# The down weights' three quarters move from GpSimd's DMA queue to SyncE's

## The chip, the cores and the metric

The kernel runs on one core of one Trainium2 chip. The metric is the device time of one execution in microseconds (us). A core has TensorE (PE, with its weight loads as PEld), VectorE (DVE), ScalarE (ACT), GpSimd (POOL) and SyncE (SP). SP computes nothing in this kernel; it issues DMAs. Its DMAs stand in the profile as queue q1 (hardware_dynamic), those that GpSimd issues as queue q0 (software_dynamic).

## The reference, cut to what matters

Two transformer blocks follow one another on 256 tokens of width 1024, all in fp32. What matters here is the feed-forward part of each, with D_FF = 2816 in the first block and 4096 in the second:

```python
# first block
g = h @ w_gate; u = h @ w_up
x = x + (silu(g) * u) @ w_down
# second block
hid = square(relu(n2 @ w_up)); mlp_out = hid @ w_down
h = h + rms_norm_2(mlp_out, norm_mlp_post)
```

Ahead of each feed-forward part stand norms, projections and attention, which the change does not touch.

## The kernel before, in words

Every fp32 operand is split into a rounded part ("hi") and the rest ("lo"), and each product is three matmuls: hi by hi, hi by lo, lo by hi. ACT rounds a weight block, DVE subtracts ("cuts") the lo part, PE multiplies.

Most weights come in "fills" of 512 KB. `sync_program` issues them in one written order on SP's queue, into four raw buffers `w_raw`; fill k waits until fill k-4 has been cut (L524), which frees its buffer. Each is rounded in `round_fill` (L1431) and cut in `cut_fill` (L2163).

The down weights come in another way. A "pair" is 256 rows of w_down by its 1024 columns. `quarters` lays a pair out as four quarters of 128x512. The product of a pair with the hidden rows is formed as a two by two product with seven instead of eight block products, which needs sums of quarters. So a pair is loaded by three DMAs, all on GpSimd's queue:

- `load_twice(q)` (L3349) writes the fourth quarter twice into `pair_t` (512 KB; shown as pair_sums).
- `load_pair(q)` (L3359) writes the three others into `pair_raw[i]` (768 KB). There are two such buffers, i = 0 (shown as pair_raw) and i = 1 (a part of `tmp`), used in turn. It waits until all three parts of pair q-2 have been cut, since pair q-2 lay in the same buffer.
- `add_pair(q)` (L3365) waits for the first to land, and adds quarters 0 and 1 onto it in the DMA (512 KB read, with accumulate).

ACT rounds a pair in three parts (`round_pair`, L1770): part 0 the three quarters, part 1 the two sums of the DMAs, part 2 two more sums that DVE has made (L2644, L2650). DVE cuts each part (`cut_pair`, L2628). The last pair of the first block and the last two of the second are "quartered": multiplied plainly, without sums. Pairs 0 to 10 belong to the first block (PAIRS1 = 11, LAST1 = 10), pairs 11 to 26 to the second (FIRST2 = 11, LAST2 = 26).

Every engine runs a written, in-order program. In the two feed-forward loops PE does for each pair its up products (L972: four fills a pair in the first block, `up1`, two in the second, `up2`), and the down products of an earlier pair (L1018); quartered pairs are multiplied on L1037. ACT takes the finished up products out of PSUM in `take_up` (L1808) or `take_hidden` (L2081), between its roundings, and PE waits for that (`up_taken`) before it writes the same bank again. In the second block's loop DVE's order for pair q, in iteration i = q - FIRST2 + 1, is

```python
cut_pair(q, 0); sum_pair(q); cut_hidden(q); sum_pair_rest(q)
cut_pair(q, 1)
cut_fill(k)        # k = first fill of up2 + 2 i + 4
cut_pair(q, 2)
cut_fill(k + 1)
```

and in the first block's loop, iteration i = q + 1, with f the first fill of up1, it ends in `cut_fill(f+4i+5)`, `cut_hidden`, `cut_pair(q, 1)`, `cut_pair(q, 2)`, `scale_gate`, `cut_fill(f+4i+6)`.

Of the kernel before, what the change touches and what calls it, by code (L numbers as in the profile page):

```python
# [40 lines left out]
PAIRS1, PAIRS2 = D_FF // (2 * P), D_FF2 // (2 * P)  # L41
# [95 lines left out]
class Weights:  # L137
# [82 lines left out]
    def used(self, name):  # L220
# [18 lines left out]
inverted_a ratio_b dens_b summed_b  # L239
x_added  # L240
spread_done spread_copied gate_scaled acted hidden_done hidden_rounded hidden_cut hidden_summed up_taken
pair_landed0 pair_landed1 twice_landed0 twice_landed1 pair_added0 pair_added1 pair_summed pair_rounded pair_cut pair_used product_done quarter_done first_copied mixed_read formed
v_gelued v_centred v_mean v_root v_scaled v_done u_done spatial_done gated_u
rows2_copied rows2_done v2_act v2_dve scored2 masked gmax_done smax_done
exped2 turned2 copied2_act copied2_dve attended2 yb_done gate_summed sigmoided
# [1 line left out]
vector_step pool_step  # L247
""".split()
Semaphores = namedtuple("Semaphores", SEMAPHORES + ["w_landed", "x_landed", "turned_landed", "post_landed", "stored", "pair_landed",
                                                   "twice_landed", "pair_added"])  # L250


def program(nc, a, out):
    with ExitStack() as ctx:
        T = Names()
        sems = {name: ctx.enter_context(nc.semaphore(name)) for name in SEMAPHORES}
        S = Semaphores(w_landed=[sems[f"w_landed{r}"] for r in range(RAW_SLOTS)],
                       x_landed=[sems[f"x_landed{t}"] for t in range(TILES)],
                       turned_landed=[sems[f"turned_landed{n}"] for n in range(KC // 2)],
                       post_landed=[sems[f"post_landed{t}"] for t in range(TILES)],  # L260
                       stored=[sems[f"stored{t}"] for t in range(TILES)],
                       pair_landed=[sems[f"pair_landed{n}"] for n in range(2)],
                       twice_landed=[sems[f"twice_landed{n}"] for n in range(2)],
                       pair_added=[sems[f"pair_added{n}"] for n in range(2)], **sems)
        allocate(nc, ctx, T)
        W = Weights(a)
        sync_program(nc, a, out, T, S, W)
        tensor_program(nc, T, S, W)
        scalar_program(nc, a, out, T, S, W)
        vector_program(nc, T, S, W)  # L270
        pool_program(nc, a, T, S, W)
# [167 lines left out]
LAST1, FIRST2, LAST2 = PAIRS1 - 1, PAIRS1, PAIRS1 + PAIRS2 - 1  # L439
# [3 lines left out]
def pair_parts(q):  # L443

    return 3 * q - sum(p < q for p in QUARTERED)


def pairs_summed(q):

    return q - sum(p < q for p in QUARTERED)  # L450


def pairs_used(q):

    return q - sum(p < q for p in QUARTERED)


def quarter_place(q, y):


    buf = pair_place(q)[0]
    return (1 - buf, y + 4) if q == LAST2 and y < 3 else (buf, y)


def pair_loads(q):

    return 16 * sum(pair_place(p)[1] == pair_place(q)[1] for p in range(q + 1))


def pair_adds(q):  # L470

    return 16 * sum(pair_place(p)[1] == pair_place(q)[1] for p in range(q + 1) if p not in QUARTERED)


def pair_place(q):

    i = q if q <= LAST1 else q - FIRST2
    return (i + 1) % 2, i % 2
# [12 lines left out]
def rows_of(out):  # L491

    return out[0].rearrange("(m s r) d -> s m r d", s=TILES, r=2)
# [12 lines left out]
def sync_program(nc, a, out, T, S, W):  # L506
    sp = nc.sync
    rows_out = rows_of(out)

    sp.dma_start(T.w_raw[:, 0:1, 0:WIDE], W.half).then_inc(S.half_landed, 16)  # L510
    for k, pieces in enumerate(W.fills):
        r = k % RAW_SLOTS
        if 0 < k < KC // 2:
            sp.dma_start(T.xt[:, 2 * k:2 * k + 2, :], a["turned"][:, 2 * k:2 * k + 2, :]).then_inc(S.turned_landed[k], 16)
        if k == RAW_SLOTS:
            sp.dma_start(T.vectors[:], a["vectors"]).then_inc(S.vectors_landed, 16)
        if k == RAW_SLOTS + 2:
            sp.dma_start(T.small[:], a["small"]).then_inc(S.small_landed, 16)
            sp.dma_start(T.xm[:], a["meta_tokens"]).then_inc(S.meta_landed, 16)
            sp.dma_start(T.rope1m[:], a["rope1m"]).then_inc(S.small_meta_landed, 16)  # L520
            for t in range(TILES):
                sp.dma_start(T.x[:, t, :], a["x"][0, t * P:(t + 1) * P, :]).then_inc(S.x_landed[t], 16)
        if k >= RAW_SLOTS:
            sp.wait_ge(*W.cut(S, k - RAW_SLOTS))  # L524
        for view, src in pieces:
            sp.dma_start(view(T.w_raw[:, r, :]), src).then_inc(S.w_landed[r], 16)
    for t in range(TILES):
        for half in range(2 - t):
            cols = slice(half * WIDE, (half + 1) * WIDE)
            sp.wait_ge(S.x_posted, 4 + 2 * t + half + 1)  # L530
            sp.dma_start(rows_out[t][:, :, cols], T.x[:, t, cols]).then_inc(S.stored[t], 16)
    for t in range(TILES):
        sp.wait_ge(S.stored[t], 32)
# [881 lines left out]
def scalar_program(nc, a, out, T, S, W):  # L1415
    act, bank = nc.scalar, T.bank
# [334 lines left out]
    def round_pair(q, part):  # L1751

        buf, i = pair_place(q)
        if part == 0:
            act.wait_ge(S.pair_landed[i], pair_loads(q))
            if q == 1:
                act.wait_ge(S.w_used, W.first["up1", 2])
            elif q == FIRST2:
                act.wait_ge(S.quarter_done, 4)
            elif q == FIRST2 + 1:  # L1760
                act.wait_ge(S.w_used, W.first["up2", 4])
            elif q > 1:
                act.wait_ge(S.pair_used, pairs_used(q - 1))
        elif part == 1:
            act.wait_ge(S.pair_added[i], pair_adds(q))
        else:
            act.wait_ge(S.pair_summed, pairs_summed(q) + 1)
        places, src = ((slice(0, 3), T.pair_raw[i]), (slice(3, 5), T.pair_t[:, i]),
                       (slice(5, 7), T.pair_raw[i][:, 0:3:2, :]))[part]
        act.activation(T.pair_hi[buf][:, places, :], src, ACT.Copy).then_inc(S.pair_rounded, 1)  # L1770

    def round_quarters(q, part):

        i = pair_place(q)[1]
        if part == 0:
            act.wait_ge(S.pair_landed[i], pair_loads(q))
            act.wait_ge(S.pair_used, pairs_used(LAST2 - 2 if q == LAST2 else q - 1))
        else:
            act.wait_ge(S.twice_landed[i], pair_loads(q))
            if q == LAST2:  # L1780
                act.wait_ge(S.product_done, 2 * len(MIXED))
        buf, y = quarter_place(q, 3 * part)
        n, src = ((3, T.pair_raw[i]), (1, T.pair_t[:, i, 0:1, :]))[part]
        act.activation(T.pair_hi[buf][:, y:y + n, :], src, ACT.Copy).then_inc(S.pair_rounded, 1)
# [35 lines left out]
    f = W.first["up1", 0]  # L1820
# [277 lines left out]
    f = W.first["up2", 0]  # L2098
# [14 lines left out]
    for i in range(2, PAIRS2 - 1):  # L2113
        q = FIRST2 + i - 1
        k = f + 2 * i + 4
# [1065 lines left out]
def pool_program(nc, a, T, S, W):  # L3181
    pool = nc.gpsimd
# [156 lines left out]
    def load_twice(q):  # L3339

        i, n = pair_place(q)[1], 1 if q in QUARTERED else 2
        if q == 0:
            pool.wait_ge(S.cut_done, CUT["h2"] + 4)
        elif q == FIRST2:
            pool.wait_ge(S.attended2, TILES * HEADS2)
            pool.wait_ge(S.x_added, 12)
        elif q not in (1, FIRST2 + 1):
            pool.wait_ge(S.pair_cut, pair_parts(q - 2) + 2)
        pool.dma_start(T.pair_t[:, i, 0:n, :], W.pairs[q][:, 3:4, :].broadcast_to([P, n, WIDE])).then_inc(S.twice_landed[i], 16)  # L3349

    def load_pair(q):
        i = pair_place(q)[1]
        if q == 1:
            pool.wait_ge(S.x_squared, 4)
        elif q == FIRST2 + 1:
            pool.wait_ge(S.x_squared, 8)
        elif q not in (0, FIRST2):
            pool.wait_ge(S.pair_cut, pair_parts(q - 1))
        pool.dma_start(T.pair_raw[i], W.pairs[q][:, 0:3, :]).then_inc(S.pair_landed[i], 16)  # L3359

    def add_pair(q):

# [2 lines left out]
        pool.dma_start(T.pair_t[:, i], W.pairs[q][:, 0:2, :], accum_op=ALU.add).then_inc(S.pair_added[i], 16)  # L3365

    load_twice(0)
    load_pair(0)
    load_twice(1)
    add_pair(0)  # L3370
    add_pair(1)
    load_pair(1)
    load_const(0)
    for q in range(2, PAIRS1):
        load_twice(q)
        load_pair(q)
        if q < LAST1:
            add_pair(q)
        if q - 1 < CONST_DMAS:
            load_const(q - 1)  # L3380
# [17 lines left out]
    pool.dma_start(T.bg[1][:], a["norm_mlp_post_2"][0:1, :].broadcast_to([P, D])).then_inc(S.post_landed[1], 16)  # L3398
    pool.wait_ge(S.w_used, W.first["o", 1])
    load_twice(FIRST2)  # L3400
    load_pair(FIRST2)
    load_twice(FIRST2 + 1)
    for t in range(TILES):
        pool.wait_ge(S.post_mean, t + 1)
# [2 lines left out]
    add_pair(FIRST2 + 1)  # L3407
    pool.wait_ge(S.x_mean, 4)
    root(T.row_scale[:, 3, :]).then_inc(S.x_root, 1)
    load_pair(FIRST2 + 1)  # L3410
    for q in range(FIRST2 + 2, LAST2 + 1):
        load_twice(q)
        load_pair(q)
        if q not in QUARTERED:
            add_pair(q)
    for t in range(TILES):
# [20 lines left out]
```

## Time and profile before

| | |
|---|---|
| median of 3 runs | 741.71 us (741.19 to 744.46) |
| the profiled execution | 742.65 us, its span 741.3 us |
| busy PE, DVE, ACT, POOL | 97%, 76%, 58%, 20% of the span |
| DMA | 149.34 MB, mean 201 GB/s |
| queue q1 (SP) | 96.68 MB, 38.6% of the 16 DMA engines' span |
| queue q0 (GpSimd) | 51.39 MB, 25.4% |
| first feed-forward loop | about 141 to 313 us |
| second feed-forward loop | about 562 to 735 us |

A row of the timeline gives the start and the duration of an instruction, and in brackets how long its engine had been idle before it and what ended that. A DMA instruction's duration is the time to issue it; the time "to landing" is from its issue until its data are there.

### The profile page before, as it was taken

To read this page: it belongs to the slowest core of one execution; us is meant where nothing else is said; L and a number is where in the kernel's file an instruction comes from. 1 tells how busy PE (TensorE), PEld (TensorE's weight loads), DVE (VectorE), ACT (ScalarE), POOL (GpSimd) and SP (SyncE) were. 2 spreads that over 40 slices of the span, in tenths; PEclk is the share of its full clock that TensorE was granted. 3 is DMA by queue.
4 is the path that set the end of the run, shared out by engine and by line. 5 is a ranking of instruction groups with operands and counts; after the bars stand their busy time and mean duration, and the time that the engine had idled before them with its cause. 6 is when DMAs were issued, how large, how long until landed. Compare 5 with 4: busy or idle time off the path is not lost.

```text
span 741.3 us, 11216 instructions
## 1 busy us (share of the span) xinstructions
PE 720.9 (97%) x4322; PEld 625.3 (84%) x4322; DVE 561.9 (76%) x817; ACT 432.9 (58%) x610; POOL 150.0 (20%) x200
## 2 busy tenths in 40 slices
PE   6999999999999999999999999999999999999996
PEld 5877778999999999888888888888778989999995
DVE  5899695689888778966747654675758899988875
ACT  6756763567665566476443444564356777767652
POOL 3867551312211110001110000000312122211200
PEclk9999999999999999999999999999999999999999
DMA  9642233699988886256536643374569799999721
GB/s 311 217 138 86 61 134 114 224 296 331 313 265 260 262 258 219 79 174 223 172 112 197 187 152 118 113 241 129 174 222 277 205 300 300 296 294 267 199 80 57
DMA packets 51750, 149.34 MB, mean 201 GB/s; under 512 B 4993, under 2 KB 6225, under 8 KB 51697
## 3 DMA queue, kind: packets, MB, share of 16 engines
q1 hardware_dynamic: 38672, 96.68, 38.6%
q0 software_dynamic: 12592, 51.39, 25.4%
q8 instruction: 34, 0.56, 0.3%
q10 hardware_dynamic: 432, 0.56, 0.2%
q14 instruction: 20, 0.16, 0.1%
HBM read 147.49 MB, written 1.05 MB: 200 GB/s over the span
## 4 chain that ended last, share of the span: by engine, by line
PE 84%; DVE 8%; DMA 5%; ACT 1%; issue 1%; POOL 0%; SPq 0%; DVEq 0%; ACTq 0%
PE psum L972 24%; PE psum L549 23%; PE psum L1018 14%; PE psum L602 11%; PE psum L1037 2%; DMA pair_sums<-in_down 2%; DVE w_lo L2163 2%; DMA w_raw<-in_w_in 2%; PE psum L776 1%; PE psum L697 1%; PE psum L642 1%; PE psum L727 1%; PE psum L1181 1%; DMA w_raw<-in_w_out 1%; DVE w_lo L2628 1%
## 5 line engine op out<-in xcount | busy, mean ns | idle before, releaser
L2163 DVE TENSOR_TENSOR w_lo<-w_raw,w_hi 128x1024 fp32r<-128x1024 f32 x171 | 209.9, 1237 | 31.6 <-ACT w_hi L1431 31.1
L1431 ACT ACTIVATE w_hi<-w_raw 128x1024 fp32r<-128x1024 f32 x177 | 184.6, 1055 | 47.0 <-DMA w_raw<-in_w_in 38.5
L972 PE MATMUL psum<-h_hi,w_hi 128*128 128x256 f32 x608 | 169.7, 283 | 2.3 <-ACT up_rows L2081 1.6
L972 PE MATMUL psum<-h_hi,w_lo 128*128 128x256 f32 x608 | 169.0, 282 | 0.0
L972 PE MATMUL psum<-h_lo,w_hi 128*128 128x256 f32 x608 | 163.3, 282 | 0.0
L972 PEld LDWEIGHTS psum<-h_hi,w_hi 128*128 128x128 f32 x608 | 114.4, 188 | 4.6 <-ACT up_rows L2081 2.1
L972 PEld LDWEIGHTS psum<-h_hi,w_lo 128*128 128x128 f32 x608 | 114.5, 188 | 0.0
L972 PEld LDWEIGHTS psum<-h_lo,w_hi 128*128 128x128 f32 x608 | 111.2, 188 | 1.3 <-DVE h_lo L2183 0.2
L549 PE MATMUL psum<-w_hi,h_hi 128*128 128x512 f32 (+1 forms) x240 | 94.5, 394 | 0.0
L549 PE MATMUL psum<-w_hi,h_lo 128*128 128x512 f32 (+1 forms) x240 | 92.9, 387 | 0.0
L549 PE MATMUL psum<-w_lo,h_hi 128*128 128x512 f32 (+1 forms) x240 | 92.9, 387 | 0.0
L549 PEld LDWEIGHTS psum<-w_hi,h_lo 128*128 128x128 f32 x240 | 45.1, 188 | 10.0
L602 PE MATMUL psum<-w_hi,h_hi 128*128 128x512 f32 x128 | 52.7, 412 | 0.4 <-DVE tmp L2896 0.4
L549 PEld LDWEIGHTS psum<-w_lo,h_hi 128*128 128x128 f32 x240 | 45.2, 188 | 9.3
L549 PEld LDWEIGHTS psum<-w_hi,h_hi 128*128 128x128 f32 x240 | 45.2, 188 | 9.2
L602 PE MATMUL psum<-w_lo,h_hi 128*128 128x512 f32 x128 | 50.5, 394 | 0.0
L3349 POOL DMA_DIRECT2D pair_sums<-in_down x27 | 19.2, 712 | 137.2 <-DVE pair_lo L2628 59.2
L602 PE MATMUL psum<-w_hi,h_lo 128*128 128x512 f32 x128 | 46.7, 395 | 0.0
L1808 ACT ACTIVATE up_rows<-psum 128x512 f32<-128x512 f32 x22 | 13.1, 594 | 53.1 <-PE psum L972 53.1
L1770 ACT ACTIVATE w_hi<-tmp 128x1536 fp32r<-128x1536 f32 (+1 forms) x24 | 30.5, 1270 | 19.0 <-DVE tmp L2650 9.9
L3365 POOL DMA_DIRECT2D pair_sums<-in_down x24 | 21.2, 882 | 94.6 <-DMA pair_sums<-in_down 94.6
L1770 ACT ACTIVATE pair_hi<-pair_raw 128x1536 fp32r<-128x1536 f32 (+1 forms) x24 | 30.5, 1273 | 16.4 <-DVE pair_raw L2650 9.7
(346 smaller groups left out, 1392.7 us busy)
## 6 DMA issues: line engine op xcount, KB each, us to landing
w_raw<-in_w_in SPq DMA_DIRECT2D x77, 512.0 KB, 4.6
w_raw<-in_up SPq DMA_DIRECT2D x76, 512.0 KB, 6.2
pair_sums<-in_down POOLq DMA_DIRECT2D x48, 512.0 KB, 6.9
pair_raw<-in_down POOLq DMA_DIRECT2D x14, 768.0 KB, 7.9
tmp<-in_down POOLq DMA_DIRECT2D x13, 768.0 KB, 8.1
w_raw<-in_w_out SPq DMA_DIRECT2D x16, 512.0 KB, 3.7
w_raw<-in_w_branch_a SPq DMA_DIRECT2D x4, 512.0 KB, 4.1
w_raw<-in_w_branch_b SPq DMA_DIRECT2D x4, 512.0 KB, 4.8
```

Source lines behind the costliest of these rows:

```text
L549: mm = pe.matmul(bank[b][:, 0:width], x[:, kc, t * P:(t + 1) * P], y[:, h * width:(h + 1) * width], start=first and n == 0, stop=last and ...
L602: mm = pe.matmul(out, x[:, kc, t * P:(t + 1) * P], y, start=n == 0 and i == 0, stop=last and i == 2)
L642: mm = pe.matmul(bank[7][0:32 + META, :], T.meta_stack[:, kc, :], y, start=kc == 0 and n == 0, stop=kc == KC - 1 and n == 1)
L972: mm = pe.matmul(out, x, y[:, kc, :], start=kc == 0 and n == 0, stop=kc == KC - 1 and n == last_pass)
L1018: mm = pe.matmul(bank[b][:], u, v, start=first and n == 0, stop=last and n == 2)
L1037: mm = pe.matmul(bank[b][:], u, v, start=first and b == 7 and c == 0 and n == 0, stop=last and c == 1 and n == 2)
L1431: act.activation(T.w_hi[:, W.slot[k], :], T.w_raw[:, k % RAW_SLOTS, :], ACT.Copy).then_inc(S.w_rounded, 1)
L1770: act.activation(T.pair_hi[buf][:, places, :], src, ACT.Copy).then_inc(S.pair_rounded, 1)
L1808: act.activation(T.rows[:, j % 2, :].rearrange("p (c n) -> p c n", c=2), src, ACT.Copy).then_inc(S.up_taken, 1)
L2163: dve.tensor_tensor(T.w_lo[:, W.slot[k], :], T.w_raw[:, k % RAW_SLOTS, :], T.w_hi[:, W.slot[k], :], ALU.subtract).then_inc(S.w_cut, 1)
L3349: pool.dma_start(T.pair_t[:, i, 0:n, :], W.pairs[q][:, 3:4, :].broadcast_to([P, n, WIDE])).then_inc(S.twice_landed[i], 16)
L3365: pool.dma_start(T.pair_t[:, i], W.pairs[q][:, 0:2, :], accum_op=ALU.add).then_inc(S.pair_added[i], 16)
```

## The change

`load_pair` is split in two. The first two pairs of each block (0, 1, 11, 12) stay on GpSimd's queue, under the name `load_first`, with the same waits, and count on semaphores of their own (`first_landed`). All other pairs (2 to 10 and 13 to 26) are loaded by SP, between its fills, with the same wait for the cuts of pair q-2. `ahead` says ahead of which fill: f+4q+6 in the first block (f the first fill of up1), and in the second the first fill of up2 + 2(q-11) + 7. Where that fill doesn't exist (pairs 24, 25, 26), the loads follow the last fill. `pair_there` gives ACT the semaphore and count of a pair. `load_twice` and `add_pair` are as before.

```diff
+FIRSTS = (0, 1, FIRST2, FIRST2 + 1)
+def pair_there(S, q):
+    i, same = pair_place(q)[1], FIRSTS if q in FIRSTS else [p for p in range(q + 1) if p not in FIRSTS]
+    return (S.first_landed if q in FIRSTS else S.pair_landed)[i], 16 * sum(p <= q and pair_place(p)[1] == i for p in same)
 ...
 def sync_program
+    def load_pair(q):
+        i = pair_place(q)[1]
+        sp.wait_ge(S.pair_cut, pair_parts(q - 1))
+        sp.dma_start(T.pair_raw[i], W.pairs[q][:, 0:3, :]).then_inc(S.pair_landed[i], 16)
+    ahead = {W.first["up1", 0] + 4 * q + 6: q for q in range(2, PAIRS1)}
+    ahead.update({W.first["up2", 0] + 2 * (q - FIRST2) + 7: q for q in range(FIRST2 + 2, LAST2 + 1)})
     for k, pieces in enumerate(W.fills):
+        if k in ahead:
+            load_pair(ahead[k])
 ...
+    for k in sorted(ahead):
+        if k >= len(W.fills):
+            load_pair(ahead[k])
 ...
 round_pair and round_quarters, part 0
-            act.wait_ge(S.pair_landed[i], pair_loads(q))
+            act.wait_ge(*pair_there(S, q))
 ...
 pool_program
-    def load_pair(q):
+    def load_first(q):
         i = pair_place(q)[1]
         if q == 1:
             pool.wait_ge(S.x_squared, 4)
         elif q == FIRST2 + 1:
             pool.wait_ge(S.x_squared, 8)
-        elif q not in (0, FIRST2):
-            pool.wait_ge(S.pair_cut, pair_parts(q - 1))
-        pool.dma_start(T.pair_raw[i], W.pairs[q][:, 0:3, :]).then_inc(S.pair_landed[i], 16)
+        pool.dma_start(T.pair_raw[i], W.pairs[q][:, 0:3, :]).then_inc(S.first_landed[i], 16)
 ...
     for q in range(2, PAIRS1):
         load_twice(q)
-        load_pair(q)
         if q < LAST1:
             add_pair(q)
 ...
     for q in range(FIRST2 + 2, LAST2 + 1):
         load_twice(q)
-        load_pair(q)
         if q not in QUARTERED:
             add_pair(q)
```

## Rows read from the trace of the kernel before

**Rows 1.** Busy time by stretch, first block's loop and second block's loop: start:end, length, busy by engine.
```profile
158.00:299.50 141.50, 141.09 (x1019) 133.21 (x1020) 119.54 (x157) 88.71 (x110) 22.98 (x34) 1.00 0.86 277
563.00:607.50 44.50, 43.01 (x302) 39.83 (x300) 41.57 (x54) 33.58 (x42) 9.66 (x13) 1.00 0.88 260
607.50:723.80 116.30, 116.15 (x760) 106.26 (x761) 103.74 (x122) 79.85 (x89) 21.62 (x31) 1.00 0.80 237
```
**Rows 2.** The chain of waits from 595 us: start, length, what.
```profile
602.02 1.68 DVE w_lo L2628
...
607.02 0.59 ACT up_rows L2081
...
607.65 5.96 PE psum L972 x48
...
713.25 5.69 PE psum L972 x48
```
**Rows 3.** All waits, 563 to 724 us: who for whom, us in total, times, longest.
```profile
POOL tmp L3359 <- DVE w_lo L2628: 10.0, 7, 1.5
ACT w_hi L1770 <- DMA tmp<-in_down: 1.8, 1, 1.8
PE psum L972 <- ACT up_rows L2081: 1.6, 1, 1.6
```
**Rows 4.** DVE timeline, 588 to 591 us: the cuts that free buffers.
```profile
588.02 1.22 DVE L2163 TENSOR_TENSOR w_lo<-w_raw,w_hi 128x1024 fp32r<-128x1024 f32 x1
589.16 1.22 DVE L2628 TENSOR_TENSOR w_lo<-tmp,w_hi 128x1024 fp32r<-128x1024 f32 x1
590.29 1.22 DVE L2163 TENSOR_TENSOR w_lo<-w_raw,w_hi 128x1024 fp32r<-128x1024 f32 x1
```
**Rows 5.** Issues of SP and POOL, and the time to landing of the load at 590.67.
```profile
589.27 0.33 SPq L526 DMA_DIRECT2D w_raw<-in_up  x1
590.67 0.56 POOL L3359 DMA_DIRECT2D tmp<-in_down  x1 [1.54 <-DVE w_lo L2628]
591.54 0.33 SPq L526 DMA_DIRECT2D w_raw<-in_up  x1
609.72 0.56 POOL L3359 DMA_DIRECT2D tmp<-in_down  x1 [1.53 <-DVE w_lo L2628]
...
DMA to landing us min/median/max: 9.7/9.7/9.7
```
**Rows 6.** ACT timeline: pair rounding, and the fill of 591.54 rounded.
```profile
588.92 1.47 ACT L1770 ACTIVATE pair_hi<-pair_raw 128x1536 fp32r<-128x1536 f32 x1
600.36 1.49 ACT L1770 ACTIVATE w_hi<-tmp 128x1536 fp32r<-128x1536 f32 x1 [1.82 <-DMA tmp<-in_down]
608.17 1.05 ACT L1431 ACTIVATE w_hi<-w_raw 128x1024 fp32r<-128x1024 f32 x1
```
**Rows 7.** DMA issues of two windows, KB and us to landing: fills of 589.27, 591.54.
```profile
w_raw<-in_up SPq DMA_DIRECT2D x1, 512.0 KB, 6.4
...
w_raw<-in_up SPq DMA_DIRECT2D x1, 512.0 KB, 9.0
```
**Rows 8.** The second block's first moved pair: its issue by POOL, SP's fill, DVE's cut.
```profile
575.24 0.56 POOL L3359 DMA_DIRECT2D pair_raw<-in_down  x1 [0.45 <-DVE pair_lo L2628]
578.39 0.33 SPq L526 DMA_DIRECT2D w_raw<-in_up  x1
592.41 1.75 DVE L2628 TENSOR_TENSOR pair_lo<-pair_raw,pair_hi 128x1536 fp32r<-128x1536 f32 x1
```
**Rows 9.** Busy time by stretch, second block, last two columns DMA share and GB/s.
```profile
589.00:600.40 11.40, 11.40 (x78) 10.46 (x78) 11.30 (x14) 7.35 (x10) 2.51 (x5) 1.00 0.91 264
```
**Rows 10.** First block: pair 3's load by POOL, its rounding by ACT, last pair's wait.
```profile
174.75 0.55 POOL L3359 DMA_DIRECT2D tmp<-in_down  x1 [0.42 <-DVE w_lo L2628]
188.92 1.48 ACT L1770 ACTIVATE w_hi<-tmp 128x1536 fp32r<-128x1536 f32 x1
716.49 1.49 ACT L1784 ACTIVATE pair_hi<-tmp 128x1536 fp32r<-128x1536 f32 x1 [0.61 <-DMA tmp<-in_down]
```

More of the change, by code:

```diff
@@ L241 @@
 spread_done spread_copied gate_scaled acted hidden_done hidden_rounded hidden_cut hidden_summed up_taken
-pair_landed0 pair_landed1 twice_landed0 twice_landed1 pair_added0 pair_added1 pair_summed pair_rounded pair_cut pair_used product_done quarter_done first_copied mixed_read formed
+pair_landed0 pair_landed1 first_landed0 first_landed1 twice_landed0 twice_landed1 pair_added0 pair_added1 pair_summed pair_rounded pair_cut pair_used product_done quarter_done first_copied mixed_read formed
 v_gelued v_centred v_mean v_root v_scaled v_done u_done spatial_done gated_u
@@ L249 @@
 Semaphores = namedtuple("Semaphores", SEMAPHORES + ["w_landed", "x_landed", "turned_landed", "post_landed", "stored", "pair_landed",
-                                                   "twice_landed", "pair_added"])
+                                                   "first_landed", "twice_landed", "pair_added"])
 def program(nc, a, out):
@@ L262, in program @@
                        pair_landed=[sems[f"pair_landed{n}"] for n in range(2)],
+                       first_landed=[sems[f"first_landed{n}"] for n in range(2)],
                        twice_landed=[sems[f"twice_landed{n}"] for n in range(2)],
@@ L1775, in round_quarters @@
         if part == 0:
-            act.wait_ge(S.pair_landed[i], pair_loads(q))
+            act.wait_ge(*pair_there(S, q))
             act.wait_ge(S.pair_used, pairs_used(LAST2 - 2 if q == LAST2 else q - 1))
@@ L3367, in pool_program @@
     load_twice(0)
-    load_pair(0)
+    load_first(0)
     load_twice(1)
@@ L3371, in pool_program @@
     add_pair(1)
-    load_pair(1)
+    load_first(1)
     load_const(0)
@@ L3400, in pool_program @@
     load_twice(FIRST2)
-    load_pair(FIRST2)
+    load_first(FIRST2)
     load_twice(FIRST2 + 1)
@@ L3409, in pool_program @@
     root(T.row_scale[:, 3, :]).then_inc(S.x_root, 1)
-    load_pair(FIRST2 + 1)
+    load_first(FIRST2 + 1)
     for q in range(FIRST2 + 2, LAST2 + 1):
         load_twice(q)
-        load_pair(q)
         if q not in QUARTERED:
```

## The prediction

> **What bounds the kernel now.** I read the busy time by stretch first, because it says how much there is to win. In the two feed-forward loops PE is busy 141.09 of 141.50 us, 43.01 of 44.50 and 116.15 of 116.30 [rows 1]: 0.41 + 1.49 + 0.15 = 2.05 us of idle time in all the stretches that hold a moved load. Matmuls bound both loops, at the full granted clock (1.00 in all three rows, the 2.4 GHz level). The chain of waits says the same: from 607.65 to 713.25 us, ten pairs of the second block, it runs over PE alone, which is 10.56 us a pair [rows 2].
>
> The one gap worth naming is the 1.6 us in which PE waits for ACT's up_rows at 607 us [rows 3]. The chain before it lies on DVE (the cut at 602.02 is on it, then ACT at 607.02) [rows 2]: DVE is busy 11.30 of 11.40 us from 589.00 to 600.40 [rows 9]. So that gap is made by DVE's amount of work, not by a load. The list of waits then shows whether the moved loads are late: in the whole second loop ACT waited for one of them once, 1.8 us, at 600.36 [rows 3, 6]. Its rounding ended at 600.36 + 1.49 = 601.85, and DVE took up the cut at 602.02 [rows 2], so even that late load was 0.17 us early where it counts. This is the tightest place in the kernel for this change; everything below turns on it. I call that load pair 14 (it is issued at 590.67), and the one before it, issued at 575.24, pair 13.
>
> **The change part by part.**
>
> *POOL's side.* 23 issues of 0.56 us leave POOL, 12.9 us, with their waits (10.0 us for the seven of one buffer [rows 3]). POOL is on no part of the path in these stretches (22.98 of 141.50 us busy, 21.62 of 116.30 [rows 1]). The add that follows on its queue still waits for the doubled quarter to land, later than the moved load was issued. It no longer has 768 KB ahead of it in queue q0, so it may land sooner; but no wait of DVE for it is among those of the loop, so sooner is worth nothing. Value 0.
>
> *SP's side, the wait.* SP now waits for the cut of part 2 of pair q-2, and its later fills queue behind that wait; ACT, DVE and PE would wait for those fills. The written order answers this. In iteration i DVE cuts fill k, then part 2, then fill k+1 (588.02, 589.16, 590.29) [rows 4]. SP issues a fill when the first is done (589.27), another when the last is done (591.54) [rows 5], and the moved load stands between them, with a wait that ends at 589.16 + 1.22 = 590.38, before the second fill's own. The wait delays no fill. The first block has the same order (part 2 lies between `cut_fill(f+4i+5)` and `cut_fill(f+4i+6)`). The issue itself is 0.33 us, in a gap of 591.54 - 589.27 = 2.27 us: hidden. And POOL issued at 590.67, 0.3 us after the cut, so SP is not later. Value 0.
>
> *The exception, pair 13.* Its cuts are done by 575.24, where POOL issued it. SP must first issue the fill ahead of it, which it does at 578.39 [rows 8]; so this one load goes out at 578.39 + 0.33 = 578.72, 3.5 us later than before. ACT rounds it at 588.92, but DVE does not take it up before 592.41 [rows 6, 8], so it may land until 592.41 - 1.49 = 590.9 us: 12.2 us after its issue. The slowest load that I show took 9.7 us [rows 5]. By that it lands at 588.4 and costs nothing.
>
> *The order within SP's queue.* Before, fill (589.27), pair load (590.67) and fill (591.54) shared the DMA engines from two queues; now all three are in one. The trace shows nothing of how a 768 KB load between two fills behaves. The bounds: at best it lands sooner than its 9.7 us, because the second fill no longer competes with it, and nothing is gained, since DVE is busy to 602.02. At worst the queue serves one DMA at a time and gives each its old time: 6.4 us for the fill [rows 7], then 9.7, so it lands at 589.27 + 6.4 + 9.7 = 605.4. I take a value near the first end. All three were done by 591.54 + 9.0 = 600.5 us before [rows 5, 7], in a stretch where the engines' share was 0.91 [rows 9]; a new order among the same bytes puts the pair load second instead of last, so it lands no later than 600.5 if the rate stays, against the 602.02 - 1.49 = 600.53 that DVE allows. I expect about 599. The second fill goes last instead. It is rounded at 608.17 [rows 6], 7.7 us after it landed; served wholly after the other two it would land at 605.4 at best and at 605.4 + 6.4 = 611.8 by the worst end. Value 0, upper end with the rivals.
>
> What the Trainium skill says here (DMA: Bandwidth & Descriptors, "Queues, rings and completion order"): each DMA engine takes turns between the queues that have work, a packet at a time. By that rule SP's queue would get about half of the 264 GB/s [rows 9] while GpSimd's has work, so 1.31 MB of fill and pair would take 9.9 us and end at 589.27 + 9.9 = 599.2 us, again ahead of 600.53. The same page ("Issuing engines are not separate DMA queues") says that a DMA's issuer changes only the issuing time. Neither changes the sum; no row before the change shows either.
>
> *The first block.* There the room is larger: pair 3 is issued at 174.75 and rounded at 188.92 [rows 10], 14.2 us. Between the preceding fill's issue and the load's lie at least two cuts of 1.22 us [rows 4], so even the worst end leaves 6.4 + 9.7 - 2.4 = 13.7 us. Value 0. *The end:* ACT waited 0.61 us for pair 26 before 716.49 [rows 10], while PE had 48 matmuls from 713.25 to 718.94 before it [rows 2]. No fill is left in SP's queue by then, and its issue is at most 0.3 us sooner. Value 0.
>
> **The sum**: 0 on POOL, 0 on SP, 0 for pair 13, 0 for the order. Against the profiled execution, 742.65 us with a span of 741.3, the change is 0; that execution lies 0.94 us above the median of 741.71, to which the forecast is carried over: 741.7 us. 0.5% (3.7 us) is about what a measurement of this kernel can tell from no change.
>
> **The rivals.**
> 1. *One stall as the second block's loop starts.* Pair 14 lands behind the fill, somewhat late, and DVE waits at 602.02 once, every microsecond past 600.53 being one of PE's. For: the room is 0.17 us, and pair 13, 3.5 us late, pushes traffic into the same time. Against: its bytes were done by 600.5 before. With 2 us late it gives 743.7; the loop absorbs the rest, since DVE's round of pairs (19.05 us for two, 590.67 to 609.72 [rows 5]) is shorter than PE's 21.1.
> 2. *The queue makes every pair late; this one is slower.* A buffer's round is the landing time plus 19.05 - 9.7 = 9.35 us of rounding, cutting and issue. It decides over PE as soon as landing takes more than 21.1 - 9.35 = 11.8 us. The worst end is 605.4 - 590.5 = 14.9; halfway between is 13.35, a round of 22.7 us, 11.35 a pair against 10.56. Ten pairs (14 to 23, those with fills around them) cost 7.9 us, and the first stall 590.5 + 13.35 + 1.49 - 602.02 = 3.3: 11.2 us, so 753 us. The worst end gives 4.9 + 10 x 1.57 = 20.6 us, 762. For it: one queue must now carry fills and pairs. Against it: q0 has lost the same bytes, so q1's share should grow.
> 3. *Faster, by the gaps.* Loads and adds land sooner, and ACT reaches its up_rows before 607.02. For: ACT's 1.8 us of waiting goes. Against: the chain there is DVE's. All of the idle time is 2.05 us, so at most 739.7, which is still within 0.5%.
> 4. *The change does not do what it says:* SP's loads go out later than POOL's in more places than pair 13. The order of cuts excludes it unless a fill ahead is held up; the effect would be rival 1's.
>
> **How the numbers follow.** Forecast 0.76, rival 1 (with 4) 0.10, rival 2 0.07, rival 3 0.07. Of the forecast's own spread and rival 3 I give 0.03 to a measured gain over 0.5%, and of the forecast and rival 1 0.02 to a loss over it; with rival 2 that is faster 0.03, same 0.88, slower 0.09. The range goes down to 740.2, three quarters of the idle time, and up to 741.7 + 3.3 = 745.0, rival 1 with the halfway landing. It leaves out rival 2 and the outermost of the others.
>
> **What would show it.** Right: PE's idle time in the three stretches within half a microsecond of 2.05; SP's moved loads at about 590.4, 599.9 and so on, 0.3 us before POOL's; pair 13 at 578.7; pair 14 landed by 600.5; the fills behind the loads landing later by some microseconds with no wait of ACT for them; the gap at 607 us still after DVE. Wrong: waits of ACT part 0 for a load on several pairs, with landing over 11.8 us (rival 2); one longer gap near 602 us (rival 1); the gap at 607 us gone (rival 3).

## The result, and the profile after

The changed kernel is slower: 748.17 us (median of 5 runs, 747.01 to 753.36) against 741.93 us (5 runs, 741.19 to 744.46), a ratio of 1.0093 with a 95% interval of 1.0073 to 1.0113. Run again beside later kernels it gave 750.4 us, ratio 1.009 (1.0062 to 1.0118). Its profiled execution is its slowest, 753.36 us with a span of 752.1 us, so the profile shows a loss of 10.7 us where the medians show 6.2. One run is left out of every time and ratio below: a run of e8 that took 1190.33 us at a granted clock of 0.558.

The stretches that answer to [rows 1] (start:end, length, busy by engine, granted clock, DMA share, GB/s):

```profile
158.00:299.50 141.50, 141.50 (x1024) 133.63 (x1023) 119.47 (x156) 88.68 (x109) 18.11 (x25) 1.00 0.88 278
563.00:607.50 44.50, 43.06 (x296) 40.07 (x294) 40.17 (x51) 32.16 (x38) 7.11 (x8) 0.98 0.81 250
607.50:723.80 116.30, 108.15 (x691) 97.81 (x692) 95.47 (x111) 74.15 (x81) 15.70 (x20) 0.99 0.80 233
```

The first block lost nothing; PE is now idle for 8.15 us of the third stretch, where it was idle for 0.15. The chain of waits (start, length, what) shows what it waits for. Up to 597 us it runs over DVE, as before; where [rows 2] had PE alone from 607.65 us on, it now has:

```profile
597.98 8.09 DMA pair_sums<-in_down
606.06 0.29 issue
606.35 0.89 POOL pair_sums L3388
607.25 0.26 issue
607.50 9.66 DMA pair_sums<-in_down
617.16 0.29 issue
617.45 0.59 POOL pair_sums L3388
618.04 11.46 DMA pair_sums<-in_down
629.50 0.29 issue
629.79 0.59 POOL pair_sums L3388
630.38 10.47 DMA pair_sums<-in_down
```

Each DMA in this chain is a doubled quarter (`load_twice`, now L3374), each POOL piece the issue of an add (L3388). The kernel's lines have moved by 22 to 25 against the rows before. GpSimd's own timeline says why they follow one another (in brackets the idle time before and what ended it):

```profile
606.35 0.89 POOL L3388 DMA_DIRECT2D pair_sums<-in_down  x1 [7.65 <-DMA pair_sums<-in_down]
607.50 0.73 POOL L3374 DMA_DIRECT2D pair_sums<-in_down  x1 [0.26 <-DVE w_lo L2653]
617.45 0.89 POOL L3388 DMA_DIRECT2D pair_sums<-in_down  x1 [9.22 <-DMA pair_sums<-in_down]
618.04 1.03 POOL L3374 DMA_DIRECT2D pair_sums<-in_down  x1
629.79 0.89 POOL L3388 DMA_DIRECT2D pair_sums<-in_down  x1 [10.71 <-DMA pair_sums<-in_down]
630.38 1.04 POOL L3374 DMA_DIRECT2D pair_sums<-in_down  x1
```

GpSimd waits for the doubled quarter of pair q, issues its add, and only then can it issue the doubled quarter of pair q+1; from 618.04 on it does so at once, with no bracket, the cut being done already. That is a closed loop of landing + 0.29 + 0.59 = landing + 0.88 us a pair. PE needs 10.56 us a pair [rows 2], so the loop decides as soon as a doubled quarter takes more than 9.68 us to land. How long it takes is in the next rows: GpSimd's doubled quarters and adds between 598 and 690 us, of the kernel before and then of the changed one.

```profile
L3349 POOL DMA_DIRECT2D pair_sums<-in_down x10: 732/735/735, 597.9 to 688.9; - x10
DMA to landing us min/median/max: 4.1/6.8/7.6
L3365 POOL DMA_DIRECT2D pair_sums<-in_down x9: 867/873/882, 604.8 to 685.5; - x9
DMA to landing us min/median/max: 5.7/6.5/7.8
```

```profile
L3374 POOL DMA_DIRECT2D pair_sums<-in_down x9: 730/1032/1038, 598.0 to 688.3; - x9
DMA to landing us min/median/max: 8.1/10.5/11.8
L3388 POOL DMA_DIRECT2D pair_sums<-in_down x8: 880/887/892, 606.4 to 687.7; - x8
DMA to landing us min/median/max: 5.1/7.0/9.8
```

From 6.8 us the doubled quarter went to 10.5, past 9.68. From 607.50 to 687.74 us seven rounds of the chain take 11.46 us each on average. Who waits in consequence, between 560 and 752 us (who for whom, us in total, times, longest), where [rows 3] had one wait of 1.8 us for a load and 1.6 us of PE:

```profile
POOL pair_sums L3388 <- DMA pair_sums<-in_down: 108.4, 13, 11.0
ACT w_hi L1795 <- DMA pair_sums<-in_down: 19.3, 5, 5.7
DVE tmp L2669 <- DMA pair_sums<-in_down: 15.9, 5, 4.8
PE psum L997 <- ACT up_rows L2106: 9.6, 5, 3.1
```

Those are 8.0 us more of PE waiting. A further part of the loss in the profiled execution is TensorE's clock. After one of these waits, of 2.5 us, PE's up products took

```profile
701.05 7.53 PE psum L997 x48
```

where the same 48 matmuls took 5.69 us before [rows 2]. The granted clock was 0.50 from 702 to 704 us, the 1.2 GHz level (behind the longest wait, 3.1 us before 654.96, it did not fall), where the kernel before had 1.00 from 560 to 740 us. That is 1.84 us, so 9.8 of the 10.7 us are placed. The fall behind the 0.98 of the second stretch (0.50 from 562 to 564 us) cost nothing: PE resumes at 607.70 us as against 607.65.

And the loads that were moved? Pair 14's, the answer to [rows 5]:

```profile
590.45 0.33 SPq L525 DMA_DIRECT2D tmp<-in_down  x1
DMA to landing us min/median/max: 7.6/7.6/7.6
```

It landed at 598.05, 2.3 us sooner than before. This moved load did well; the doubled quarter, which stayed where it was, lands later.

### The profile page after: what moved, and what is told of

It reads as the page before. It is cut to its first block, busy times and chain, and to the rows that moved or that the text cites. A ratio compares the mean times of both kernels' runs of the same rounds, so it can differ in the third digit from the quotient of the medians.

```text
span 752.1 us, 11216 instructions
## 1 busy us (share of the span) xinstructions
PE 725.2 (96%) x4322; PEld 628.9 (84%) x4322; DVE 561.5 (75%) x817; ACT 433.0 (58%) x610; POOL 137.5 (18%) x177
## 4 chain that ended last, share of the span: by engine, by line
PE 76%; DMA 14%; DVE 6%; issue 2%; ACT 1%; POOL 1%; SPq 0%; DVEq 0%; ACTq 0%
PE psum L574 23%; PE psum L997 21%; DMA pair_sums<-in_down 12%; PE psum L627 12%; PE psum L1043 8%; PE psum L1062 2%; DMA w_raw<-in_w_in 2%; PE psum L801 1%; PE psum L722 1%; DVE w_lo L2188 1%; PE psum L667 1%; PE psum L752 1%; PE psum L1206 1%; PE psum L703 1%; PE psum L773 1%
## 5 line engine op out<-in xcount | busy, mean ns | idle before, releaser
L997 PE MATMUL psum<-h_hi,w_hi 128*128 128x256 f32 x608 | 171.6, 285 | 9.7 <-ACT up_rows L2106 9.6
L997 PE MATMUL psum<-h_hi,w_lo 128*128 128x256 f32 x608 | 170.9, 284 | 0.0
L997 PEld LDWEIGHTS psum<-h_hi,w_hi 128*128 128x128 f32 x608 | 116.1, 191 | 13.1 <-ACT up_rows L2106 11.7
L997 PEld LDWEIGHTS psum<-h_hi,w_lo 128*128 128x128 f32 x608 | 116.1, 191 | 0.0
L3388 POOL DMA_DIRECT2D pair_sums<-in_down x24 | 21.5, 894 | 186.4 <-DMA pair_sums<-in_down 186.4
L2653 DVE TENSOR_TENSOR w_lo<-tmp,w_hi 128x1536 fp32r<-128x1536 f32 (+1 forms) x24 | 35.7, 1487 | 3.5 <-ACT w_hi L1795 3.5
L3374 POOL DMA_DIRECT2D pair_sums<-in_down x27 | 21.4, 793 | 89.3 <-DVE w_lo L2653 36.0
L1795 ACT ACTIVATE w_hi<-tmp 128x1536 fp32r<-128x1536 f32 (+1 forms) x24 | 30.5, 1270 | 10.8 <-DVE tmp L2675 5.4
```

The costliest lines, as they stand in the source:

```text
L997: mm = pe.matmul(out, x, y[:, kc, :], start=kc == 0 and n == 0, stop=kc == KC - 1 and n == last_pass)
L2653: dve.tensor_tensor(T.pair_lo[buf][:, places, :], src, T.pair_hi[buf][:, places, :], ALU.subtract).then_inc(S.pair_cut, 1)
```

## The experiments

The experiments ran in four groups (e1 to e4, e5 to e8, e9 to e12, e13 and e14). The runs of a group shared one chip and the runs of the kernel before, whose median was 742.94, 742.64, 743.15 and 743.29 us; across groups, compare the ratios. Theory: the loop on GpSimd, closed by a doubled quarter that lands late. Rivals: a wait of SP that holds up fills; the moved loads themselves; the late pair 13; too many bytes in SP's queue, whatever the order.

**Where the loss lies.** e1 is the changed kernel again.

> The changed kernel again, beside those that follow. Its profile has the chain of waits in the second block on the doubled quarter (load_twice, 9.3 to 11.8 us to landing) and GpSimd issuing, one right after the other, an add and the next doubled quarter. Theory: this in-order loop on GpSimd (wait for the doubled quarter, 0.9 us to issue the add, next doubled quarter) bounds the second block, at landing + 0.9 us a pair, where PE needs 10.56. All theories expect 747 to 750 us here.

750.4 us, ratio 1.009 (1.0062 to 1.0118), 0.4 us over what was expected. The loop is in its profile too: the doubled quarters land after 10.2 us (median).

```diff
 e2: only the first block's pairs on SP
-FIRSTS = (0, 1, FIRST2, FIRST2 + 1)
+FIRSTS = (0, 1) + tuple(range(FIRST2, LAST2 + 1))
 e3: only the second block's
+FIRSTS = tuple(range(PAIRS1)) + (FIRST2, FIRST2 + 1)
```

> SP loads the three quarters in the first block only; pairs 13 to 26 are loaded by GpSimd as before. The theory of the loop on GpSimd expects 742 us, as before, since a pair of the first block gives PE 16.4 us. A rival that says any wait of SP for a pair's cut delays fills expects a third of the loss or more, 744.

742.6 us, ratio 1.0008 (0.9989 to 1.0027).

> SP loads the three quarters in the second block only. The theory of the loop on GpSimd expects the whole loss here, 747 to 749 us.

750.87 us, ratio 1.0108 (1.0073 to 1.0142). That is 2 us over what was expected, within the spread of its runs (746.04 to 755.01). The whole loss is the second block's. In the first block SP's new waits cost nothing (e2); for the second block e7, below, says the same.

**Opening the loop.** e4 takes the doubled quarters off GpSimd's program:

```diff
+    def load_twice(q):          # in sync_program
+        sp.wait_ge(S.pair_cut, pair_parts(q - 2) + 2)
+        sp.dma_start(T.pair_t[:, i, 0:n, :], ...).then_inc(S.twice_landed[i], 16)
     for k, pieces in enumerate(W.fills):
+        if k in doubled:        # up2: first fill + 2 (q - FIRST2) + 6
+            load_twice(doubled[k])
         if k in ahead:
             load_pair(ahead[k])
 pool_program, both loops
-        load_twice(q)
```

> SP also loads the doubled quarter, ahead of the fill before the three quarters; GpSimd only adds. If the in-order loop on GpSimd is the cause (the next doubled quarter waits behind the add, which waits for the doubled quarter), this opens it: a doubled quarter goes out at the cut, and the time is 741 to 743 us. If it is that SP's queue holds too much and each of its DMAs lands later, the doubled quarter is now in that queue too and lands after 10 us or more; add 6 us and the rounding, and the round of a buffer is over 21 us: 748 us or more.

742.52 us (12 runs, 741.42 to 743.96), ratio 0.9993 (0.9977 to 1.001). SP's queue now holds still more, and each of its DMAs lands sooner than in the changed kernel; the DMA issues from 607 to 690 us (count, KB each, median us to landing):

```profile
w_raw<-in_up SPq DMA_DIRECT2D x16, 512.0 KB, 6.3
pair_sums<-in_down SPq DMA_DIRECT2D x9, 512.0 KB, 5.4
pair_sums<-in_down POOLq DMA_DIRECT2D x8, 512.0 KB, 7.1
tmp<-in_down SPq DMA_DIRECT2D x4, 768.0 KB, 6.3
```

That ends the rival of too many bytes in SP's queue. PE's gap before 607.49 us is still there, 1.7 us, and no other wait of PE for ACT's up_rows is left. e5 tried to open the loop by order alone:

```diff
     for q in range(FIRST2 + 2, LAST2 + 1):
         load_twice(q)
-        if q not in QUARTERED:
-            add_pair(q)
+        if q > FIRST2 + 2 and q - 1 not in QUARTERED:
+            add_pair(q - 1)
```

> As the changed kernel, but in the second block GpSimd issues the doubled quarter of pair q before the add of pair q-1; every transfer stays on its queue. If GpSimd's in-order loop (doubled quarter waits behind the add) bounds, this opens it as well as moving the doubled quarter did: 741 to 744 us. If the queues' sharing alone makes the doubled quarter and the add late, nothing changes: 747 to 751.

807.26 us, ratio 1.086 (1.0822 to 1.0899): my expectation was wrong by 65 us. The order opens one loop and closes a longer one. The add of pair q-1 now stands behind the wait for the cut of part 1 of pair q-2, and the cut of part 1 of pair q-1 needs that add:

```profile
651.39 0.71 POOL pair_sums L3374
652.10 11.82 DMA pair_sums<-in_down
...
664.02 0.69 DVE pair_raw L2669
...
666.32 1.15 DVE pair_lo L2653
...
667.75 0.71 POOL pair_sums L3374
```

This is a piece of its chain of waits: 16.36 us a pair (651.39 to 667.75), of which the add's landing is 11.8. So e5 says nothing of the queues' sharing, but it shows how much one in-order queue with two waits can cost.

e7 leaves the order and shortens the transfer in the loop: from pair 13 on the last quarter is loaded once, not twice, and the second sum is made on old contents.

```diff
-        i, n = pair_place(q)[1], 1 if q in QUARTERED else 2
+        i, n = pair_place(q)[1], 1 if q in QUARTERED or q > FIRST2 + 1 else 2
```

> As the changed kernel, but from pair 13 on the last quarter is loaded once and not twice (256 KB in place of 512 KB), so the second sum is made on the old contents. The loop on GpSimd is the landing of this DMA plus 0.9 us: with half its bytes it lands at least 2 us sooner, below the 9.7 us that PE's 10.56 us a pair allows, and the time is 741 to 743. If another transfer is what bounds (the three quarters, a fill), the time stays within 2 us of the changed kernel's.

742.22 us, ratio 0.9991 (0.9971 to 1.0011). The doubled quarter, now half as large, lands after 3.7 us (median), and everything else recovers with it: fills after 5.6 us where the changed kernel has 9.7 in the same stretch, the three quarters after 6.1 where it has 9.2 and 10.1. Half the doubled quarter's bytes are gone as well, so this alone does not say what the loop did to the others; e12, below, has all the bytes and the same recovery. SP's waits and their order are those of the changed kernel, so the rival of SP's waits falls here for the second block too. e8 tests the one exception that the prediction had seen:

```diff
-FIRSTS = (0, 1, FIRST2, FIRST2 + 1)
+FIRSTS = (0, 1, FIRST2, FIRST2 + 1, FIRST2 + 2)     # pair 13 stays on GpSimd's queue
```

> As the changed kernel, but pair 13, the one that SP issues 3.5 us later than GpSimd did, stays on GpSimd's queue. If the late pair 13 pushes the traffic together and starts the loss, it goes: 742 to 744. The theory of the loop on GpSimd expects 747 to 751, since the loop closes in the pairs after it.

749.75 us (6 runs, 743.79 to 753.24), ratio 1.0079 (1.0043 to 1.0115). Pair 13 is not the cause.

**Why the doubled quarter lands late.** It now competes with 768 KB in SP's queue, which before lay behind it in its own queue. But bytes alone don't say how the two queues share. A row (the bytes of one partition) of a fill is 4 KB, of the three quarters 6 KB. e6, e9, e13 and e10 change the rows:

```diff
 e6: three DMAs of 256 KB, rows of 2 KB
-        sp.dma_start(T.pair_raw[i], W.pairs[q][:, 0:3, :])
+        for n in range(3):
+            sp.dma_start(T.pair_raw[i][:, n:n + 1, :], W.pairs[q][:, n:n + 1, :])
 e9: as e6, and each fill of up2 in two DMAs of 2 KB rows
 e13: one DMA of 768 KB, its quarter rows 512 bytes apart in memory
+        sp.dma_start(T.pair_raw[i], W.apart[q][:, :, 0:WIDE])
 e10: two DMAs of 64 partitions, rows of 6 KB
+        for n in range(2):
+            rows = slice(64 * n, 64 * n + 64)
+            sp.dma_start(T.pair_raw[i][rows], W.pairs[q][rows, 0:3, :])
```

> As the changed kernel, but each moved pair is loaded by three DMAs of 256 KB (rows of 2 KB) in place of one of 768 KB (rows of 6 KB), in both blocks. If the engines take turns between the two queues by row, a 6 KB row against 4 KB ones gives SP's queue the larger part, and with 2 KB rows the doubled quarter lands sooner than its 10 us and the time falls to 742 to 745. If it is only the bytes in SP's queue, it stays at 747 to 751.

> As e6, and the fills of the second feed-forward part are loaded by two DMAs of 2 KB rows each in place of one of 4 KB rows, so that nothing in SP's queue there has rows over 2 KB. If the engines give a queue its turn by row, the doubled quarter lands sooner than e6's 8.6 us (7 us or less, as in the kernel before) and the time is that of the kernel before, 742. If e6 gained only because its load came in three DMAs, the fills add nothing: 743 to 744, landing 8 to 9 us.

> As the changed kernel, with one DMA of 768 KB for a pair, but its source lies apart in memory (each 2 KB quarter row followed by 512 bytes that are not read), so that it can only be read in rows of 2 KB. If the row's size sets how much SP's queue takes from GpSimd's, it behaves as e6 did: 742 to 745, doubled quarter landing at 8 to 9 us. If e6's gain came from issuing three DMAs in turn, it stays at 747 to 751 with 10 us or more.

> As the changed kernel, but each moved pair is loaded by two DMAs of 64 partitions each: rows stay 6 KB, DMAs are 384 KB. By the theory of turns by row it stays at 747 to 751 with the doubled quarter landing after 9.5 us or more. If it is the size of a DMA that counts, it falls to 743 to 745 as e6 did.

| | time, us | range of the runs | ratio to before (95%) | doubled quarter lands after, us (min/median/max, 598 to 690 us) |
|---|---|---|---|---|
| changed (e1) | 750.40 | 745.53 to 752.54 | 1.009 (1.0062 to 1.0118) | 8.1/10.2/11.4 |
| e6 | 743.18 | 741.26 to 746.43 | 1.0000 (0.9978 to 1.0023) | 6.7/8.6/10.8 |
| e9 | 742.34 | 741.28 to 743.41 | 0.9979 (0.9963 to 0.9996) | 7.8/8.7/10.3 |
| e13 | 743.04 | 741.25 to 749.31 | 1.0001 (0.9978 to 1.0024) | 6.9/9.7/10.3 |
| e10 | 765.73 | 761.72 to 769.45 | 1.0292 (1.0241 to 1.0343) | 10.1/12.5/14.4 |

e13 is the clean one: one DMA, the same bytes, the same partitions, only shorter rows, and its ratio is 1.0001 in place of 1.009. So the length of a row in SP's queue bears on the kernel's time. That it acts through the doubled quarter's landing fits but is weaker: 9.7 us at the median against 10.2, and 10.3 at most against 11.4, from one profile each, where I had expected 8 to 9. e3, with the whole loss, has a median of 9.7 too (7.2/9.7/12.1). With 9.7 us e13 stands right on the bound of 9.68, and its runs spread over 8 us, which would fit a loop at its bound. e9's time came out as expected, but not its landing: I had said 7 us or less, and it is 8.7, no better than e6. The rows of the fills matter less than those of the pairs, or not at all. e10 was meant as a control, with 747 to 751 us expected, and is not one: DMAs on 64 partitions use more of the engines for the same bytes (second row; share of the engines by MB 52.2/11.40 = 4.6, against 43.3/13.30 = 3.3 in the changed kernel, both from 607 to 690 us), so its loss has a cause of its own. It therefore does not settle whether smaller DMAs help as such; e13 shows that they are not needed.

```profile
q1 hardware_dynamic: 3144, 13.30, 43.3%
```

```profile
q1 hardware_dynamic: 2776, 11.40, 52.2%
```

The Trainium skill (DMA: Bandwidth & Descriptors, "Queues, rings and completion order") has each engine take turns between queues a whole packet at a time. e13's time agrees, e9's landing gives it no support: from 607 to 690 us queue q1 has 3144 packets for 13.30 MB in the changed kernel, 5213 for 13.95 MB in e13 (ratio 1.0001), and 8064 for 14.68 MB in e9, where the doubled quarter still lands after 8.7 us as against 8.6 in e6.

e11 and e12 change the two other things that the doubled quarter meets: the add just ahead of it in its own queue, and the order in SP's.

```diff
 e11: from pair 13 on the add's DMA overwrites instead of adding
-        ..., W.pairs[q][:, 0:2, :], accum_op=ALU.add)
+        ..., W.pairs[q][:, 0:2, :], **({} if q > FIRST2 + 1 else dict(accum_op=ALU.add)))
 e12: the three quarters after the second fill of an iteration, up2 only
-    ahead.update({W.first["up2", 0] + 2 * (q - FIRST2) + 7: q ...
+    ahead.update({W.first["up2", 0] + 2 * (q - FIRST2) + 8: q ...
```

> As the changed kernel, but from pair 13 on the add's DMA writes without adding (same bytes read, no accumulate), so the sums are wrong. The doubled quarter is issued 0.6 us behind the add in the same queue; if the accumulate is slow in that queue, the doubled quarter lands by 2 us or more sooner than 10.2 and the time is 741 to 744. If an accumulating DMA costs the queue no more than a plain one, nothing changes: 747 to 751.

741.93 us (10 runs, 741.32 to 742.61), ratio 0.9981 (0.9966 to 0.9997): the doubled quarter lands after 8.8 us, the plain copy after 5.5 where the add took 7.0. So the accumulate just ahead of it is a part of the late landing, 1.4 us against e1's 10.2 (I had expected 2 or more).

> As the changed kernel, but in the second block SP issues a pair's three quarters after the second fill of the iteration and not before it, about 1.1 us later. The bytes in SP's queue beside the doubled quarter are the same, only their order differs, so the loop on GpSimd stays closed: 747 to 752. If the place between the fills matters (the doubled quarter meets a 512 KB fill first and not 768 KB), the time falls to 743 to 746.

742.31 us, ratio 0.9987 (0.9966 to 1.0009). I had thought this order would not matter. It cures nearly everything: 607 to 690 us, DMA issues and the waits of GpSimd:

```profile
w_raw<-in_up SPq DMA_DIRECT2D x16, 512.0 KB, 5.8
tmp<-in_down SPq DMA_DIRECT2D x4, 768.0 KB, 6.9
...
POOL pair_sums L3388 <- DMA pair_sums<-in_down: 46.2, 8, 6.8
POOL pair_sums L3374 <- DVE w_lo L2653: 11.5, 4, 3.3
POOL pair_sums L3374 <- DVE pair_lo L2653: 11.3, 4, 3.5
```

The doubled quarters land after 6.6 us (5.0/6.6/7.2) as in the kernel before, and GpSimd waits for cuts again: the loop is open. SP issues the three quarters 3.5 us after GpSimd's doubled quarter (602.87 after 599.36) where the changed kernel does so 2.0 us after it (599.97 after 597.98). So the same transfers, in the same two queues, with 1.5 us' difference in one place of SP's order, land after 6.6 or after 10.5 us. That points to feedback, and this is how I read it: a late doubled quarter makes its add late; the next doubled quarter then follows that add in the queue by 0.6 us in place of some 2.7 (604.82 to 607.45 before the change), meets more of its accumulate, and lands later still: 8.09, 9.66, 11.46 us in the chain of the changed kernel. e3, which has the changed kernel's second block, shows both regimes in one execution. On GpSimd, and then the landings of its doubled quarters from 597 to 635 us and from 635.5 to 690:

```profile
626.24 0.73 POOL L3374 DMA_DIRECT2D pair_sums<-in_down  x1 [0.98 <-DVE w_lo L2653]
634.97 0.88 POOL L3390 DMA_DIRECT2D pair_sums<-in_down  x1 [8.00 <-DMA pair_sums<-in_down]
635.86 0.73 POOL L3374 DMA_DIRECT2D pair_sums<-in_down  x1
...
DMA to landing us min/median/max: 7.2/7.4/8.4
...
DMA to landing us min/median/max: 9.7/11.5/12.1
```

As long as GpSimd waits for cuts (the last bracket of that kind is at 626.24), the doubled quarters land after 7.4 us; once it no longer does, after 11.5.

**A version with both cures**, e14: the doubled quarter on SP as in e4, the three quarters after the second fill as in e12.

> The doubled quarter on SP as in e4 and, in the second block, the pair's three quarters after the second fill as in e12. Both open the loop on GpSimd; PE bounds then, so no more than the kernel before can lose to late transfers is to be had: 741.5 to 743, ratio to before 0.997 to 1.000.

742.29 us (12 runs, 741.19 to 743.98), ratio 0.9987 (0.9974 to 1.0001). No clear gain: with the loop open PE bounds, busy 92.50 of the 92.50 us from 607.50 to 700 us in e4's profile. Only e9 and e11 have intervals that end below 1, by 0.04% and 0.03%, and e11 leaves work out. e9 is the one whole kernel that may beat the one before, by 0.2%; among so many versions one can show that much by chance.

## Why the prediction was wrong

*What bounds before.* Right: PE, with 2.05 us of idle time to win. The versions that undo the loss came back to between 741.9 and 743.2 us, and of those only e9 and e11 are below the kernel before, by 0.2%. In the changed kernel PE's idle time in the three stretches is 0.00 + 1.44 + 8.15 = 9.59 us, which by the prediction's own sign is wrong.

*SP's side, the wait,* and *the exception, pair 13,* and *the first block:* right, each at 0 (e7 742.22 us with all of SP's waits; e8 749.75 us without the late pair 13, so it has no part in the loss; e2 742.6 us).

*The order within SP's queue:* right as far as it went. Pair 14 landed at 598.05, before the 600.53 that I allowed, the 599 that I expected and the 599.2 that came out by the Trainium skill's rule (DMA: Bandwidth & Descriptors, "Queues, rings and completion order"). I asked only when the moved load and the fill behind it would land.

*POOL's side: this is the step that failed.* I wrote that POOL "is on no part of the path", that the add "may land sooner" and that "sooner is worth nothing. Value 0". I counted GpSimd's busy time and looked for waits of DVE on the add, but never priced the doubled quarter, the transfer that stayed behind and now shares the engines with 768 KB more from the other queue. Nor did I follow what stands behind its wait: POOL's add, and behind that the next doubled quarter. The numbers were there. The list of [rows 3] is headed "All waits" but shows three of them; its first line was GpSimd's wait for this very transfer:

```profile
POOL pair_sums L3365 <- DMA pair_sums<-in_down: 49.9, 13, 5.1
```

The doubled quarter's 6.8 us plus 0.88 was 7.7 us a pair against 10.56, a margin of 2.9 us. The three quarters, landing after 8.1 us at the median, had 3.7 to my bound of 11.8; my 12.2 and 11.8 us were for the DMA with more room. The landing of the doubled quarter rose by 3.7 us, from 6.8 to 10.5, more than its margin. The term "POOL: 0" measured 6.2 us at the median and 10.7 in the profiled execution, of which 1.84 us are the lower clock after a wait.

*The argument that the same bytes are done by the same time* "if the rate stays" hid this. It holds for the sum, not for each transfer: the pair load won 2.3 us, and the doubled quarters lost up to 5 (11.8 at most, against 6.8 at the median before).

*Rival 2* gave 753 us, which the profiled execution happens to match. Its mechanism was another: moved loads landing over 11.8 us. From 598 to 690 us they landed after 8.3 to 11.0 us in the changed kernel, and ACT waited for them 4.8 us in the whole loop (3.7, and 1.1 for a quartered pair), against 19.3 us for the sums. It does not count as foreseen; its evidence against ("q0 has lost the same bytes, so q1's share should grow") was true (the q1 row above, 43.3% from 607 to 690 us, against 25.6% before), and was the danger.

Left open: by how much a row's length shifts the sharing (e9 shows no effect of the fills' rows on the landing, e6 and e13 one of the pairs' rows, small in e13); where the last 0.9 us of the profiled loss lie; and why the runs of the changed kernel spread over 6 to 7 us, while those of e4, e7, e9, e11 and e14 spread over 1.3 to 2.8 (e12 4.8; e2 and the kernel before have single runs at 749). That the bound is crossed in some rounds and not in others fits, but was not followed run by run.

## What to carry to other kernels

When a transfer moves to another queue, price those that stay: list each DMA that something waits for in order, with landing time plus issue against the period of the bounding engine, and take the loop with the least room first. An in-order queue that waits for its own DMA before it issues the next one is such a loop, and here it got worse by itself once it was late. If it is at its bound, move the DMA that nobody needs to hold back (e4) or let the competing one go out a little later (e12); swapping the order on the queue can close a longer loop (e5).

## What the runs showed of the hardware that I had not expected

- The row length of a load changed the kernel's time: the same 768 KB in one DMA, in rows of 6 KB or of 2 KB, gave ratios of 1.009 and 1.0001 (e1, e13). The doubled quarter's landing in the other queue differed little, 10.2 and 9.7 us.
- With the same load as two DMAs of 64 partitions the kernel took 765.7 us; the queue's share of the engines rose from 3.3% to 4.6% a MB.
- An accumulating DMA of 512 KB landed after 7.0 us, a plain one in its place after 5.5, and GpSimd needed 0.89 us to issue it, against 0.56.
- Two orders of the same DMAs, 1.5 us apart, settled into two regimes, with landings of 6.6 and 10.5 us (e12, the changed kernel); in e3 one execution went from 7.4 to 11.5.
- After a wait of 2.5 us the granted clock was 0.50 for 2 us, and 48 matmuls took 7.53 us in place of 5.69 (the changed kernel, 701 us).
